# Stream zero's feed-forward tiles between the expert slots, attention heads with fewer passes, one load per tile and stream

## The reference, cut to what matters

```python
# first block, its last part: product-key experts, 8 heads x 16 experts for each token
act = gelu(einsum('thkd,td->thk', expert_u[eidx], tb))
out = einsum('thk,thkd->td', g * act, expert_v[eidx])
x = layer_norm(ALPHA * x + gate2 * out, ln2_g, ln2_b)
# second block
for layer in range(2):
    hn = rms_norm_2(x, norm_mix_g[layer])
    x = x + (rglru_mixer(hn, ...) if layer == 0 else dsa_mixer(hn, ...))
    x = x + square(relu(rms_norm_2(x, norm_mlp_g[layer]) @ w_up[layer])) @ w_down[layer]
return rms_norm_2(x, final_norm_g)
# dsa_mixer, for each query: the best topk = 64 keys by an index score, then 16 heads
logits = einsum('bqhc,bqkc->bqhk', q_lat, c_sel) + bias
o_lat = einsum('bqhk,bqkc->bqhc', softmax(logits), c_sel)
```

## Time and profile before

| | us |
|---|---|
| runs shown | 2015.1, 2014.46, 2009.04 (median 2014.46) |
| profiled execution | 2013.02 |
| its span | 2011.2 |
| PE busy | 1805.5 (90%) |
| PE weight load busy | 1699.0 (84%) |
| DVE busy | 880.9 (44%) |
| ACT busy | 555.3 (28%) |
| POOL busy | 307.4 (15%) |
| mean granted TensorE clock | 0.975 |

### The profile page before, as it was taken

One profiled execution on the slowest core, in us unless ns is written; L12 is line 12 of the kernel. 1 busy time (PEld: TensorE's weight loads), 2 busy tenths in 40 slices (PEclk: granted clock), 3 DMA queues, 4 the chain that ended last, 5 costly groups with the idle time before them and its releaser, 6 DMA issues.

```text
span 2011.2 us, 32188 instructions
## 1 busy us (share of the span) xinstructions
PE 1805.5 (90%) x13254; PEld 1699.0 (84%) x13254; DVE 880.9 (44%) x2198; ACT 555.3 (28%) x1490; POOL 307.4 (15%) x284
## 2 busy tenths in 40 slices
PE   3999998999999788778998878799999997699998
PEld 2888887888799777778998777799999986699998
DVE  6621573332255776767867764332100335311001
ACT  0111225340133444434474443231100122211000
POOL 0100000000023445434334444000000000000000
PEclk9998999999999999999999999899999998799999
DMA  9942332233379999999999999678464340044440
GB/s 375 383 169 79 139 114 103 84 105 128 125 273 405 420 421 420 421 419 419 401 399 421 421 421 420 263 246 281 166 210 149 125 144 1 1 159 148 149 150 25
DMA packets 73441, 487.76 MB, mean 243 GB/s; under 512 B 7713, under 2 KB 14417, under 8 KB 14801
## 3 DMA queue, kind: packets, MB, share of 16 engines
q0 software_dynamic: 39168, 285.23, 34.4%
q1 hardware_dynamic: 31872, 189.49, 26.3%
q10 hardware_dynamic: 2256, 11.00, 1.4%
HBM read 484.61 MB, written 1.07 MB: 241 GB/s over the span
## 4 chain that ended last, share of the span: by engine, by line
PE 69%; DMA 17%; DVE 7%; ACT 3%; issue 3%; POOL 0%; ACTq 0%; DVEq 0%; POOLq 0%
PE PS L819 30%; PE PS L587 21%; PE PS L783 8%; DMA V<-in_peer_uv_dram,SCR 7%; DMA AUX<-in_peer_uv_dram,SCR 6%; DMA CONV<-in_peer_uv_dram,SCR 3%; PE PS L609 1%; PE PS L634 1%; DMA PROJ<-in_ada_dram 1%; DVE PROJ L1867 1%; PE PS L854 1%; PE PS L724 1%; PE PS L968 1%; PE PS L683 1%; PE PS L969 1%
## 5 line engine op out<-in xcount | busy, mean ns | idle before, releaser
L587 PE MATMUL PS<-H,ring 128*128 128x256 f32 x1408 | 316.6, 386 | 5.0 <-DVE H L1791 3.6
L587 PEld LDWEIGHTS PS<-H,ring 128*128 128x128 f32 x1408 | 271.4, 194 | 43.3 <-issue 4.3
L783 PE MATMUL PS<-PROJ,AUX 128*128 128x128 f32 x2048 | 248.8, 280 | 50.7 <-ACT PROJ L1259 50.5
L783 PEld LDWEIGHTS PS<-PROJ,AUX 128*128 128x128 f32 x2048 | 237.3, 194 | 61.0 <-ACT PROJ L1259 60.9
L783 PE MATMUL PS<-PROJ,CONV 128*128 128x128 f32 x1536 | 197.0, 290 | 52.7 <-ACT PROJ L1259 52.6
L783 PEld LDWEIGHTS PS<-PROJ,CONV 128*128 128x128 f32 x1536 | 189.2, 204 | 59.3 <-ACT PROJ L1259 59.3
L1093 POOL DMA_INDIRECT AUX<-in_peer_uv_dram,SCR x128 | 151.2, 1182 | 505.0 <-DVE SCR L1851 314.3
L1867 DVE CUSTOM_DVE_ANT_0 PROJ<-AUX,PROJ 128x1024 f32<-128x1024 f32 x128 | 156.3, 1227 | 124.0 <-DMA AUX<-in_peer_uv_dram,SCR 123.4
L819 PE MATMUL PS<-H,ring 128*128 128x128 f32 x1632 | 189.0, 275 | 0.0
L819 PEld LDWEIGHTS PS<-H,ring 128*128 128x128 f32 x1632 | 185.7, 192 | 0.2
L819 PE MATMUL PS<-PROJ,ring 128*128 128x128 f32 x1440 | 166.6, 275 | 1.9 <-DVE X L1962 1.9
(11 more groups left out here) (299 smaller groups left out, 1877.5 us busy)
## 6 DMA issues: line engine op xcount, KB each, us to landing
ring<-in_stream_dram SPq DMA_DIRECT2D x127, 1024.0 KB, 4.8
AUX<-in_stream_dram SPq DMA_DIRECT2D x48, 1024.0 KB, 4.8
AUX<-in_ada_dram POOLq DMA_DIRECT2D x16, 1024.0 KB, 10.3
AUX<-in_ada_dram ACTq DMA_DIRECT2D x4, 1024.0 KB, 12.4
PROJ<-in_ada_dram ACTq DMA_DIRECT2D x4, 1024.0 KB, 20.8
AUX<-in_peer_uv_dram,SCR POOLq DMA_INDIRECT x128
CONV<-bias_by_distance SPq DMA_DIRECT2D x1, 2048.0 KB, 14.9
CONV<-in_peer_uv_dram,SCR POOLq DMA_INDIRECT x96
```

What stands on the lines that cost most here:

```text
L587: mm = pe.matmul(acc(n, c), w[:, k, c * P:(c + 1) * P], src[:, g * DC + k, :], start=(g == 0 and k == 0 and (c == 0 or groups == 1)), stop ...
L783: mm = pe.matmul(y_chunk(t, c), UV[b][:, D + c * P:D + (c + 1) * P], DIAG[n % ND], start=(k == 0 and c % 4 == 0), stop=(k == SPT - 1), ski ...
```

## The change

1. *Order of the streams.* Stream zero's up0 (16 tiles) and down0 0 to 9 go between the expert slots: a tile at each odd n from 191 to 241, with relu, square, residual and squares at fixed slots four or five behind. After slot 255 down0 10 to 15 stand beside stream one's norms; stream one's rec_in beside stream zero's norm; stream zero's attention layer runs beside stream one's rec_out and up0 (two up0 tiles in each step of the heads); stream one's down0 beside att_out; stream one's attention beside stream zero's up1 (one tile in each step). up1 and down1 of both streams alternate, stream one behind.
2. *Loads.* Every entry has one user, so each tile is loaded once for each stream. `EARLY` is 38, `WIDER` 7: the first 38 entries use the ring's four places, the rest the ring and three AUX buffers. uk_uv gets the fourth AUX buffer and a semaphore of its own.
3. *Heads.* `shift_logits` is one `tensor_tensor_reduce` per head (add the mask, keep the maximum) and a change of the maximum's sign; `probs_exp` is one activation per head with the maximum as bias and the sum as accumulator; `normalise` is a reciprocal and a multiply. Three (stream zero) and four (stream one) buffers for the probabilities instead of two; the logits of stream one run three steps ahead.
4. *Places in SBUF.* HID, QT2, QLAT, OT, PR, PT, OL move so that the two streams have their own; the latent's squares get a place of their own (SQC). `causal` also makes what `forbid` made. In `keep_top(0)` the four residuals of stream one's rec_out stand between the rounds.

```diff
-    add("up0", range(11, 16), (0, 1))
-    add("down0", range(16), (0, 1))
...
+    add("rec_in", range(8), 0)
+    add("rec_out", range(4), 0)
+    add("up0", range(16), 0)
+    add("down0", range(16), 0)
+    add("rec_in", range(8), 1)
...
-EARLY = 12
-WIDER = 8
+EARLY = 38
+WIDER = 7
@@ tensor
+                if 191 <= n < 223 and n % 2:
+                    tile2(0, "up0", (n - 191) // 2, ready=normed(0, 1) if n == 191 else None)
+                if 223 <= n < 243 and n % 2:
+                    tile2(0, "down0", (n - 223) // 2, ready=hidden(0, 0) if n < 231 else None)
+            def front_half():
+                tile2(0, "down0", 10)
+                sum2(1, "mean", X[:, :, us(1)], lambda k: pe.wait_ge(S("y_added"), DC + k + 1))
+                tile2(0, "down0", 11)
+                square_sum(1, "ln2", "var")
+                tile2(0, "down0", 12)
+                tile2(0, "down0", 13)
+                square_sum(1, "mix0")
+                tile2(0, "down0", 14)
+                tile2(0, "down0", 15)
+                tile2(1, "rec_in", 0, ready=normed(1, 0))
...
             for q in range(4):
                 transpose_probs(0, q)
                 if q + 2 < 4:
                     logits(0, q + 2)
+                tile2(1, "up0", 7 + 2 * q)
                 attend_latents(0, q)
+                tile2(1, "up0", 8 + 2 * q)
                 head_values(0, q)
...
             for p in range(8):
                 transpose_probs(1, p)
+                if p + 3 < 8:
+                    logits(1, p + 3)
+                tile2(0, "up1", 4 + p)
                 attend_latents(1, p)
                 head_values(1, p)
@@ scalar
+                if 195 <= n < 227 and n % 2:
+                    relu_out(0, "up0", (n - 195) // 2)
+                if n in (234, 242):
+                    squares_of(0, "mix1", "down0", (n - 234) // 8)
...
+            squares(1, "mix0")
+            squares_of(0, "mix1", "down0", 3)
+            root(1, "mix0")
             def probs_exp(u, b):
-                act.wait_ge(S(f"shifted{u}"), b + 1)
-                act.activation(PR[u][b % 2], PR[u][b % 2], ACT.Exp).then_inc(S(f"exped{u}"), 1)
+                m, w = HEADS_IN[u], KEYS_OF[u]
+                act.wait_ge(S(f"top_ready{u}"), b + 1)
+                for e in range(m):
+                    p = PR[u][b % (3 + u)][:, e * w:(e + 1) * w]
+                    act.activation(p, p, ACT.Exp, bias=TOP[u][b % 4][:, e:e + 1], accum_out=SUM[u][b % 4][:, e:e + 1])\
+                        .then_inc(S(f"exped{u}"), 1)
@@ vector
+                if 196 <= n < 228 and n % 2 == 0:
+                    hidden_out(0, "up0", (n - 196) // 2)
+                if n in (233, 241):
+                    residual2(0, "down0", (n - 233) // 8)
...
+            rms2(1, "mix0", "mix_g", 0)
             did(dve.tensor_copy(XR1[:, :, 0:3], TAIL))
+            rms2(0, "mix1", "mix_g", 8)
             for c in (0, 2, 4, 6):
                 rec_conv(1, c, 2)
...
             def shift_logits(u, b):
-                p = by_head(PR[u][b % 2], u)
-                taken(dve.tensor_tensor(p, by_head(bank(("lg", u, b)), u), over(MSK[u], m), ALU.add), ("lg", u, b))
+                top = TOP[u][b % 4]
+                for e in range(m):
+                    x = slice(e * w, (e + 1) * w)
+                    ins = dve.tensor_tensor_reduce(PR[u][b % (3 + u)][:, x], bank(("lg", u, b))[:, x], MSK[u], 1.0, NEG,
+                                                   ALU.add, ALU.max, top[:, e:e + 1])
...
-                did(dve.tensor_reduce(TOP[u][b % 2], p, AX.X, ALU.max))
-                dve.tensor_tensor(p, p, spread(TOP[u][b % 2], w), ALU.subtract).then_inc(S(f"shifted{u}"), 1)
+                dve.tensor_scalar(top, top, -1.0, None, ALU.mult).then_inc(S(f"top_ready{u}"), 1)
             def normalise(u, b):
-                did(dve.tensor_reduce(SUM[u][b % 2], p, AX.X, ALU.add))
+                total = SUM[u][b % 4]
...
+                did(dve.reciprocal(total, total))
...
+            index_weights(0)
+            latent_norm(0)
+            update(1)
+            gate_update(1)
+            index_scores(0)
+            keep_top(0, lambda t: residual2(1, "rec_out", t))
+            rms2(1, "mlp0", "mlp_g", 0)
```

## The result

| | us |
|---|---|
| forecast | 1956 (1936 to 1987) |
| measured, median of 4 runs | 1953.88 (1949.21 to 1961.41) |
| kernel before beside it, median of 4 runs | 2012.39 (2009.04 to 2015.1) |
| ratio, with its 95% interval | 0.9714 (0.9678 to 0.9749) |
| profiled execution, its span | 1953.04, 1951.2 |

The changed kernel is 2.9% faster. A second set of five runs, beside a later experiment, gave 1958.27 us and a ratio of 0.9735 (0.9722 to 0.9749).

A forecast was written before the change was run, and what follows sets the result against it. DMA was taken to bound the expert slots and PE most work behind them, with waits and slow clock in the heads. 2013.0 - 92.9 + 65.3 - 51 + 22 gave 1956 us, range 1936 to 1987.

The forecast's parts named there:

- The moved tiles in the slots, +65.3: Expert slots: 26 added tile loads cost 64.8 us, one AUX refill less saves 2.5, slower mixed traffic adds 3.
- a slower mixed rate: Expert slots with tiles: a pair of slots takes 7.6 us instead of 7.48, +3 us over 26 tiles.
- -92.9: Behind the slots: 26 tiles leave full PE at 3.573 us each, saving 92.9 us.
- -51: Attention heads: all PE time lost to waits and a halved clock goes, saving 51 us.
- 22: Heads and behind the slots: new waits of 19.9 us plus 2 for the unseen and clock, bounds 10 and 45.
- The term for clock and the unseen: Heads and behind the slots: 2 us for unseen waits and for clock lost behind the new waits.
- Every tile per stream, 0: Behind the slots: 136 tile uses each become a load, 294 GB/s, at cost 0.
- A: Expert slots: mixed slots run slower, 7.87 to 8.8 us a pair, +7 to +31 us, 1963 to 1987; chance 0.12.
- B: Heads: only half the gain comes, through engine hops and a dropped clock, +26 us, about 1982; chance 0.15.
- C: Expert slots: gathers get half the DMA engines while a tile loads, 9.9 us a pair, +60, 2016; chance 0.03.
- D: Behind the slots: tile loads bind, one at a time at 4.8 us each, +167 us, 2123; chance 0.04.
- E: Whole kernel: better than 1935 us if waits behind the slots hide and slots run at PE's 7.15; chance 0.03.

The follow-up runs named there:

- slots16: Changed kernel with only up0's 16 tiles between the slots, down0 0 to 9 behind slot 255 (EARLY 28): 1966.34 us, ratio 0.9779 to the kernel before.
- slots0: Changed kernel with all 26 moved tiles behind slot 255 instead of between the slots (EARLY 12): 1986.95 us, ratio 0.9884 to the kernel before.
- all_in: Changed kernel with EARLY 42, two instruction orders turned behind the slots, and normalise and logits moved earlier in the heads: 1928.34 us, ratio 0.9591 to the kernel before.
- ring4: Changed kernel with WIDER 4, so only the ring's four places serve the weights and no AUX buffer is refilled: 1952.31 us, ratio 0.9701 to the kernel before.
- early42: Changed kernel with EARLY 42, the first AUX refill coming four ring tiles later, after the last gathers: 1949.82 us, ratio 0.9694 to the kernel before.
- heads_only: Kernel before with only the three rewritten head steps; order, loads and places as before, two buffers: 1990.44 us, ratio 0.9895 to the kernel before.

## Why the prediction was right, point by point

**What bounds it.** Right. The slots go by DMA and the rest by PE; slots16 and slots0 measured both prices separately, 2.52 and 3.44 us a tile over the 26 for 2.49 and 3.573.

**The moved tiles in the slots, +65.3.** By first gather and last dot it was +62.3 (709.6 to 771.9). The load price and the AUX refill, 25 x 2.49 = 62.3, meet that to the digit, which is luck: the same slots differ by some 3 us between executions, and the other profiles give 61 to 67. The 3 us that I added for a slower mixed rate are of the same size, so the lengths can't refute them alone; but their reason was wrong. The row at 289 GB/s, on which I rested them, was no loss of rate but the end of a supply. PE was at other work (line 854, 7.15 us from 1028.14), no buffer came free, and POOL's next gather, at 1037.34, had waited 7.95 us for PE. The forecast also spread the excess of DMA over the pairs, 7.6 us each. The pairs took 7.25, near PE's 7.15, and the excess came behind the last tile. Over the whole stage the bytes count, not the single window. The page of the Trainium skill that I weighed there ("DMA: Bandwidth & Descriptors", "Where 436 GB/s comes from", about 358 GB/s between HBM and SBUF) does not bind this core. By that figure 26 tiles would have cost 76 us, an estimate. The trace disagrees: from 1116.6 to 1301.3 the stage moves 420 GB/s, and 421 from there to 1330.

**The tiles behind the slots and the heads, -92.9 - 51 + 22 = -121.9.** It was -118.5 (726.1 to 607.6). slots0 has the same tiles behind the slots as the kernel before and takes 697.1: its -29.0 is what the heads' passes, their cover and the new order gave together, and the forecast's -51 + 22 is -29. That it agrees to the digit is luck again, since its parts were off by 2 to 5 us (below), and the -51 counts 16 records of line 942 as single that are 256 wide, 1.8 us. The 3 us that are missing lie in the last ten tiles (32.6 instead of 35.7); they are PE's busy time, as said above. The single waits were 1.90 and 3 x 1.31 in stream zero (forecast 2.0 and 3 x 1.5), 0.7 before the queries (0.5), 1.95 at stream one's first transposes (2.1), 8 x 0.56 (and no 0.15 more), 2.69 before rec_in (3.0), 2.1 before rec_out (2.1): 17.8 for 19.9. The term for clock and the unseen was 2, and the waits that all_in removes had 6.5 us of slower matmuls with them: this term was mis-sized. With both figures the 22 would have been some 24.

**Sum.** The two errors nearly cancel (-3.0 and +3.4), which is luck. The profiled execution shows 3.4 us more gain than forecast because its first stage happened to be 3.8 us shorter. Against the medians the forecast of 56.6 us stands beside 58.5 and 53 measured.

**Every tile per stream, 0.** Right as to the wait, and too cautious: ring4 shows that four places do. The number of places was not free, though. I had priced the AUX refills in the slots as 3 x 2.49 and taken them as given; early42 shows that a constant removes them.

**The rivals.** A fell with the table (420 GB/s through all the pairs, 2.5 us a tile). B fell with slots0, whose rest is 29 us shorter where B would leave 3, and no wait in the heads is over 2.0 us. C described the tail correctly (4.96 us apart while AUX tiles load, 2.45 when no tile loads; that agrees with the rule of the Trainium skill, "DMA: Bandwidth & Descriptors", "Queues, rings and completion order", that each DMA engine takes turns between the queues with work) and the pairs wrongly. D fell with ring4. E had the pairs nearly right (7.25 us for PE's 7.15) and came to nothing, because the debt followed behind them and all its waits were there.

## What to carry to other kernels

Where one stage is bound by transfers and the next by TensorE, moving a piece of TensorE work into the first is worth its matmul time less its transfer time, and both prices can be read from rows before anything is built; here 1.08 us a tile by the rows, 0.9 by the parts of the profiles and 1.2 by the medians. Where one wait ends another engine's chain, list the instructions that stand before the awaited one in that engine's order: such waits at four places, twelve waits and 15.4 us in all, could be listed by hand from the diff and went away by turning neighbours around. Look also at what starts to load when a stage's last buffers come free, for the last transfers share with it.

## What the runs showed of the hardware that I had not expected

Four tile places of 1 MB feed TensorE at full rate behind the slots: one wait of 2.3 us in some 600 us, even with 3 MB of a strided load on the same queue (2 MB of it took 14.8 us to land in ring4). And a wait costs more than itself, by an amount that varies: behind the last dot heads_only was idle 13.8 us less and 17.9 us shorter, all_in 15.4 less and 21.9 shorter, each time because the same matmuls took less time. Yet one wait of 1.95 us cost no clock in slots16 and slots0 and did in both profiles of the changed kernel.
